# A hybrid decoder step: projected tiles turned to rows in 32x32 blocks by VectorE and moved to their lanes by GpSimd, the convolution's first product on ScalarE

## The reference

```python
n = rmsnorm(h, g);  u = n @ w_in            # columns: z | xBC | dt | q | k | v
xbc_ext  = concatenate([conv_prev, xbc], axis=1)
new_conv = xbc_ext[:, -3:]                  # an output
xbc_act  = silu(b + sum(xbc_ext[:, j:j + L] * w[j] for j in range(4)))
y = ssd_chunked(x * dt, dt, A, B, C, state) + d_skip * x     # x | B | C = xbc_act
y = rmsnorm_by_group(y * silu(z)) * ssd_norm
o = rmsnorm(dilated_attention(q, k, v))     # k and v of the new tokens are outputs
h = h + concatenate([y, o]) @ w_out
h = h + moe(rmsnorm(h))                     # top 4 of 32 experts, clamped SwiGLU
return rmsnorm(h)
```

## Time and profile before

| | us |
|---|---|
| median of 3 runs | 1232.03 (1231.84 to 1236.32) |
| the profiled execution, first to last instruction | 1232.7 |
| TensorE busy (PE) | 1160.5 (94%) |
| VectorE busy (DVE) | 365.5 (30%) |
| ScalarE busy (ACT) | 250.0 (20%) |
| GpSimd busy (POOL) | 55.2 (4%) |
| chain that ended last | PE 57%, DMA 38%, DVE 2% |
| DMA | 463.58 MB, mean 376 GB/s |

### The profile page before, as it was taken

One profiled execution on the slowest core, in us unless ns is written; L12 is line 12 of the kernel. 1 busy time (PEld: TensorE's weight loads), 2 busy tenths in 40 slices (PEclk: granted clock), 3 DMA queues, 4 the chain that ended last, 5 costly groups with the idle time before them and its releaser, 6 DMA issues.

```text
span 1232.7 us, 14855 instructions
## 1 busy us (share of the span) xinstructions
PE 1160.5 (94%) x5867; PEld 506.8 (41%) x5882; DVE 365.5 (30%) x752; ACT 250.0 (20%) x496; POOL 55.2 (4%) x49
## 2 busy tenths in 40 slices
PE   9999999899999999999989898989898989898997
PEld 6777656534433434333333333333232323232332
DVE  2457335765512132221203030303122121212122
ACT  2014443627320211112011111111111111020113
POOL 0000032621000000000000000000000000000000
PEclk9999999999999999999999999999999999999999
DMA  9677557379799999999999999999999999999995
GB/s 293 207 250 256 205 183 280 135 254 417 326 426 430 426 427 430 427 430 428 427 430 428 426 431 428 427 430 429 429 429 427 429 428 427 430 427 428 429 427 247
DMA packets 64368, 463.58 MB, mean 376 GB/s; under 512 B 7704, under 2 KB 25268, under 8 KB 38380
## 3 DMA queue, kind: packets, MB, share of 16 engines
q1 hardware_dynamic: 62206, 459.02, 90.5%
q10 hardware_dynamic: 1582, 2.22, 0.5%
q0 software_dynamic: 544, 1.84, 0.4%
HBM read 455.82 MB, written 7.24 MB: 376 GB/s over the span
## 4 chain that ended last, share of the span: by engine, by line
PE 57%; DMA 38%; DVE 2%; issue 1%; ACT 1%; SPq 0%; DVEq 0%; ACTq 0%
DMA ring<-in_w 34%; PE ps L2436 21%; PE ps L1909 10%; PE ps L2460 5%; DMA own<-in_w 3%; PE ps L2354 2%; PE ps L2362 2%; PE ps L2323 2%; PE ps L2356 1%; PE ps L2194 1%; PE ps L1951 1%; PE ps L2372 1%; PE ps L2422 1%; PE ps L1985 1%; PE ps L1928 1%
## 5 line engine op out<-in xcount | busy, mean ns | idle before, releaser
L2436 PE MATMUL ps<-ring,own 128*64 128x512 f32 x1456 | 326.5, 595 | 31.4 <-DMA ring<-in_w 31.4
L2436 PEld LDWEIGHTS ps<-ring,own 128*64 128x64 f32 x1456 | 104.1, 137 | 236.0 <-issue 178.3
L1763 DVE TENSOR_SCALAR own<-ps 128x512 f32<-128x512 f32 x32 | 22.1, 692 | 556.8 <-PE ps L2436 556.8
L2436 PE MATMUL ps<-own 128*64 128x512 f32 x592 | 134.1, 594 | 11.8 <-DMA own<-in_w 11.8
L2460 PE MATMUL ps<-ring,own 128*64 128x512 f32 x592 | 133.5, 595 | 5.4 <-issue 5.2
L1909 PE MATMUL ps<-own,ring 128*128 128x288 f32 x512 | 131.4, 412 | 0.0
L1909 PEld LDWEIGHTS ps<-own,ring 128*128 128x128 f32 x512 | 96.1, 192 | 29.2 <-issue 4.5
L2460 PE MATMUL ps<-own 128*64 128x512 f32 x432 | 98.4, 595 | 3.9 <-issue 2.6
L2436 PEld LDWEIGHTS ps<-own 128*64 128x64 f32 x592 | 43.2, 137 | 95.1 <-issue 84.5
L2460 PEld LDWEIGHTS ps<-ring,own 128*64 128x64 f32 x592 | 44.0, 137 | 82.9 <-issue 72.5
L1151 ACT ACTIVATE own<-ps 64x512 f32<-64x512 f32 x60 | 35.5, 592 | 205.6 <-PE ps L2460 204.8
(11 more groups left out here) (384 smaller groups left out, 1003.1 us busy)
## 6 DMA issues: line engine op xcount, KB each, us to landing
ring<-in_w SPq DMA_DIRECT2D x128, 2048.0 KB, 38.6
own<-in_w SPq DMA_DIRECT2D x63, 2048.0 KB, 37.4
ring<-in_w_in SPq DMA_DIRECT2D x16, 1024.0 KB, 7.7
ring<-in_cache_win_k SPq DMA_DIRECT2D x8, 1024.0 KB, 5.8
ring<-in_cache_win_v SPq DMA_DIRECT2D x8, 1024.0 KB, 4.9
ring<-in_w_out SPq DMA_DIRECT2D x6, 1024.0 KB, 10.9
ring<-in_state_ssm SPq DMA_DIRECT2D x8, 512.0 KB, 7.3
out_ssm_sample<-ring SPq DMA_DIRECT2D x8, 512.0 KB, 8.6
```

Source lines behind the costliest of these rows:

```text
L1763: nc.vector.tensor_scalar(xg_o, hid[:, 0], LIMIT, None, ALU.min).then_inc(sem("glu_ready"), 1)
L2436: last = nc.tensor.matmul(ps[C * half:C * half + C, 1 + m, :], xT[:, k, C * u:C * u + C], rows[:, D * half + 512 * m:D * half + 512 * m + ...
```

## The change

- The `nat` and `conv_out` steps go: 26 times three transposes and three times four on TensorE, with their copies out of bank 2, and the waits for this bank.
- A `turn` step, or for v and z the copy out of the projection itself, is one VectorE transpose in 32x32 blocks of a 128x288 tile, into `turned_tiles` (room for two pairs of tiles). k is turned from `kT`, x and B from `xbcT` after SiLU, v and z straight from PSUM.
- After a block transpose each 32x32 block is right in itself but stands on the lanes of its columns. `blocks_to_rows` on GpSimd takes a pair of tiles and copies the blocks to the lanes of their tokens: for each of 4 groups of lanes 4 copies of 128 elements per lane and one of 64. There are 13 pairs. It signals `natural`, and VectorE waits for it before it fills the room of the pair two before.
- The convolution tails are one VectorE transpose (`tails`, 128x768) and eight GpSimd copies of 384 elements per lane.
- All x, B and C projections are copied out by ScalarE, all v and z by VectorE.
- The convolution's first product is an activation on ScalarE (scale and bias by lane), ahead of VectorE's three additions.

```diff
+TURNED = [n for n, (kind, i, _) in enumerate(TILES) if n % 2 == 0 and (kind in "kvz" or (kind == "x" and i < 10))]
+OUT_ON_DVE = [n for n, (kind, i, _) in enumerate(TILES) if kind in "vz" or (kind in "qk" and n % 2)]
+OUT_ON_ACT = [n for n in range(NT) if n not in OUT_ON_DVE]
@@ mixer_steps
         proj(9 + 2 * b)
-        back(7 + 2 * b if b < 3 else 2 * b + 5)
         steps.extend(("silu", i) for i in convs)
+        steps.extend(("turn", 12 + i) for i in convs)
@@ GpSimd
+            def blocks_to_rows(n):
+                what, j, _ = TILES[n]
+                rows, j = {"k": (k_nat, j), "v": (v, j), "z": (z, j), "x": (xs, j)}[what]
+                if what == "x" and j >= 8:
+                    rows, j = Bn, j - 8
+                pair = 2 * (TURNED.index(n) % 2)
+                if what in "vz":
+                    wait_proj_out(pool, n + 1)
+                else:
+                    pool.wait_ge(sem("blocks_ready"), sum(1 for m in TURNED if m <= n and TILES[m][0] in "kx"))
+                for i in range(4):
+                    lanes = slice(32 * i, 32 * i + 32)
+                    for q in range(4):
+                        to = rows[32 * q:32 * q + 32, 0:2, j * P:(j + 2) * P].rearrange("p c (t r) -> p c t r", t=2)[:, :, :, lanes]
+                        nc.gpsimd.tensor_copy(to, turned_tiles[lanes, pair:pair + 2, 0:SEQ].rearrange("p t (c q r) -> p q c t r", c=2, q=4)[:, q])
+                    last = nc.gpsimd.tensor_copy(rows[0:NS, 2, j * P:(j + 2) * P].rearrange("p (t r) -> p t r", t=2)[:, :, lanes], turned_tiles[lanes, pair:pair + 2, SEQ:TOK])
+                last.then_inc(sem("natural"), 1)
+                pool.wait_ge(sem("natural"), TURNED.index(n) + 1)
+            for name, src, ns in (("k", k_nat, (4, 6)), ("v", v, (8, 10))):
+                for n in ns:
+                    blocks_to_rows(n)
...
+            for n in range(12, 22, 2):
+                blocks_to_rows(n)
+            pool.wait_ge(sem("kv_out"), 64)
+            pool.wait_ge(sem("tails_ready"), 1)
...
+            pool.wait_ge(sem("score_ps"), DB)
+            blocks_to_rows(24)
+            blocks_to_rows(26)
             pool.wait_ge(sem("dt_ready"), 1)
...
+            blocks_to_rows(28)
...
             pool.wait_ge(sem("w_used"), NT // 2)
             decays_in(0)
...
+            blocks_to_rows(30)
             pool.wait_ge(sem("silu_ready"), CT)
@@ ScalarE
+                elif kind == "conv":
+                    wait_proj_out(act, 12 + i)
...
+                    nc.scalar.activation(conv_t[:, i % 2, :], xbcP[:, i, 0:XC], ACT.Identity, scale=cw[:, i, 24:25], bias=cw[:, i, 28:29]).then_inc(sem("conv_begun"), 1)
@@ VectorE
+                        moved = TURNED.index(i - i % 2) - 1
+                        if i % 2 == 0:
+                            dve.wait_ge(sem("natural"), moved)
+                        nc.vector.transpose(d3(turned_tile(i), 32), d3(src, 32)).then_inc(sem("proj_out_dve"), 1)
+                elif kind == "turn":
+                    what, j, _ = TILES[i]
+                    if i % 2 == 0 and TURNED.index(i) > 1:
+                        dve.wait_ge(sem("natural"), TURNED.index(i) - 1)
+                    if what == "x":
+                        dve.wait_ge(sem("silu_ready"), j + 1)
+                        src = xbcT[:, j, :]
...
+                    ins = nc.vector.transpose(d3(turned_tile(i), 32), d3(src, 32))
@@ VectorE, conv
-                    link(nc.vector.tensor_scalar(t, xbcP[:, i, 0:XC], cw[:, i, 24:25], cw[:, i, 28:29], ALU.mult, ALU.add))
@@ TensorE, nat
-                    turn_waits()
-                    turn[:] = [kind, i]
-                    for c in range(3):
-                        last = nc.tensor.transpose(ps[0:ROWS[c], 2, c * P:(c + 1) * P], src[:, cols(c)], ident)
-                    last.then_inc(sem("nat_ps"), 1)
```

More of the change, by code:

```diff
@@ L157, in mixer_steps @@
 def mixer_steps():
-    steps, nat = [], 0
+    steps = []
     def proj(n):
         steps.append(("proj", n))
-    def back(last, most=1):
-        nonlocal nat
-        for _ in range(most):
-            if nat < len(NAT) and NAT[nat] <= last:
-                steps.append(("nat", nat))
-                nat += 1
     for n in range(8):
         proj(n)
-        back(n - 2)
         if n == 4:
             steps.append(("qrep", 0))
+        if n == 6:
+            steps.extend([("turn", 4), ("turn", 5)])
     for b in range(DB):
@@ L181, in mixer_steps @@
         if b == 0:
-            steps.append(("krep", 0))
-        back(6 + 2 * b if b < 3 else 2 * b + 5)
+            steps.extend([("krep", 0), ("turn", 6), ("turn", 7)])
         steps.extend(("conv", i) for i in convs)
@@ L207, in mixer_steps @@
     steps.extend(("exp", i) for i in range(4, 8))
-    steps.extend([("silu", 10), ("silu", 11), ("conv_out", 0)])
+    steps.extend([("silu", 10), ("silu", 11), ("tails", 0)])
     steps.extend(("pv", t) for t in range(3))
     proj(26)
-    steps.extend([("conv_out", 1), ("ptrans", 4), ("ptrans", 5), ("conv_out", 2)])
-    back(24)
+    steps.extend([("ptrans", 4), ("ptrans", 5)])
     proj(27)
@@ L246 @@
 STEPS = mixer_steps()
-NAT_ON_DVE = [i for i in range(len(NAT)) if i < 8 and i % 2 == 0]
-NAT_ON_ACT = [i for i in range(len(NAT)) if i not in NAT_ON_DVE]
 def ring_items():
@@ L733, in _ @@
+            pool.wait_ge(sem("tails_ready"), 1)
+            for i in range(4):
+                for q in range(2):
+                    last = nc.gpsimd.tensor_copy(conv_o[32 * q:32 * q + 32].rearrange("p (m r) -> p m r", m=CT)[:, :, 32 * i:32 * i + 32], tails[32 * i:32 * i + 32, :, q, :])
+            last.then_inc(sem("conv_o"), 1)
+            pool.wait_ge(sem("conv_o"), 1)
+            pool.wait_ge(sem("score_ps"), DB)
+            blocks_to_rows(24)
+            blocks_to_rows(26)
             dA = dts[:, 48:96]
@@ L735, in _ @@
             pool.wait_ge(sem("dt_ready"), 1)
-            pool.wait_ge(sem("conv_out_ps"), 3)
-            for i in range(8, 18):
-                wait_nat_out(pool, i)
             for c in range(3):
@@ L1865, in old_round @@
                 if r == 0:
-                    for n in range(len(NAT)):
-                        wait_nat_out(pe, n)
                     pe.wait_ge(sem("Qz_ready"), 3)
@@ L1988, in _ @@
                     if i == 0:
-                        for n in range(4, 8):
-                            wait_nat_out(pe, n)
+                        wait_natural(pe, "v")
                     for b in range(4):
@@ L2011, in _ @@
                     last.then_inc(sem("dt_ps"), 1)
-                elif kind == "conv_out":
-                    wait_proj_out(pe, 14 + 4 * i)
-                    wait_proj_out(pe, 15 + 4 * i)
-                    turn_waits()
-                    turn[:] = [kind, i]
-                    for m in range(4):
-                        last = nc.tensor.transpose(ps[0:59, 2, m * P:(m + 1) * P], xbcP[:, 4 * i + m, XS0 - 3:XP], ident)
-                    last.then_inc(sem("conv_out_ps"), 1)
                 elif kind == "p_score":
```

130 lines of the change are left out of this document (36 added, 94 removed).

## The result

The changed kernel takes 1226.21 us (median of 4 runs, 1223.19 to 1227.56), the kernel before beside it 1232.9 us (4 runs, 1231.84 to 1236.32): a ratio of 0.9934 with a 95% interval of [0.9917, 0.9951]. By the ratio that is 8.1 us faster (6.0 to 10.2 by the interval); the two medians differ by 6.7 us, the spans of the two profiled executions by 7.0. The forecast was 1220.5 us, 11.6 us faster, with 1218 to 1223.5 as its own band and a range of 1215 to 1230. The measured median lies in the wide range and not in the band.

What follows compares the result with a forecast made beforehand. The expert-weight stream sets the end and starts when the mixer, bound by TensorE's order to 200 us, frees buffers. Savings 5.4 + 4.4 + 0.6 + 1.7 = 12.1, less 0.5 for GpSimd, give 1220.5 us, range 1215 to 1230.

Steps and rivals of the forecast that it cites:

- Sixteen turns at 0.335 us: TensorE before 129 us: 16 of the 26 turns, three transposes each, go and save 5.4 us.
- The waits for the shared bank: TensorE behind 129 us: waits for ScalarE over the single bank of all turns go, together 4.4 us.
- The turn beside the softmax: One later TensorE turn costs 1.35 us with its wait; 0.6 counted, since the softmax transposes need ScalarE too.
- Five turns of 0.335: Five of TensorE's last seven turns cost 0.335 us each, 1.7 us saved.
- the wait is hidden: Sample loop: VectorE's block transposes wait for ScalarE's SiLU, but TensorE wants the next keys only 9.85 us later.
- the second block transpose end 2.6 us after the odd projection: Sample loop: a copy and two SiLUs on ScalarE, then VectorE's transpose, end 2.6 us after the odd projection.
- the zeroed tile: GpSimd's memset ends at 190.3 us, VectorE's copy into its tile is due at 189.8; 0.5 us charged.
- Charging nothing: VectorE and GpSimd contending for SBUF: copies lie mostly under one-input key transposes, so no time is charged.
- A: Rival: GpSimd's queue gives part of the gain back, memset late by 2.9 to 10 us; 1226 us, chance 0.18.
- B: Rival: GpSimd becomes the bound, gain gone at 10.7 us a pair; 1245 us at 0.60 us a copy, chance 0.09.
- C: Rival: the saving isn't passed on, as something unmoved releases the first expert weights; 1232 us, chance 0.06.
- D: Rival: more is saved, the last turn, the whole 1.35 us and shorter shared-bank waits; 16 us, 1216, chance 0.05.

Runs made afterwards that it cites:

- e5: The kernel before with only the convolution's first product moved to ScalarE, turns left on TensorE: 1235.12 us against 1233.98, ratio 1.0015.
- e1: The changed kernel with VectorE taking the prompt's maxima ahead of the six convolution additions at sample 4: 1222.85 us, ratio 0.9894 to the kernel before.
- e9: The changed kernel with VectorE's block transposes moved behind the next sample's key transposes: 1225.71 us, ratio 0.9935 to the kernel before.
- e6: The changed kernel with the convolution's first product back on VectorE: 1228.16 us, ratio 0.9955 to the kernel before.
- e11: The changed kernel with 8 GpSimd copies instead of 20 for each x pair, giving other numbers there: 1225.93 us, ratio 0.9931 to the kernel before.
- e4: The changed kernel with maxima ahead of the additions, GpSimd's last z pair later, three unused TensorE products: 1223.21 us, ratio 0.9899 to the kernel before.
- e8: The changed kernel with maxima ahead of sample 4's additions and three unused TensorE products ahead of its wait: 1222.8 us, ratio 0.9917.

## Why the prediction was right, and where its sizes were off

**The size.** The direction, the mechanism and the wide range came true; the size did not. Of 11.6 us some 7 to 8 arrived, and 1226.21 us lies even above 1225.9, below which the forecast laid 0.77 of its chances. That the wide range held it is in part luck: what was lost by the wait and the low clock below stood in no term of the sum. Another part of the distance to 1220.5 us is the base: it was the median of three runs, 1232.03 us, and 37 later runs of that kernel have a median of 1234.09.

**The direction and the mechanism.** Time left TensorE's chain with the turns, and reached the end: at the second old round the changed kernel's profile is 6.9 us earlier (214.27 against 221.13), at its end 7.0. From that round to the end it is 1011.6 us before and 1011.4 after. Step by step, up to the last pattern product of the prompt (199.18 before, 189.60 after, 9.6 us earlier where 12.1 was forecast):

- Sixteen turns at 0.335 us, 5.4 us forecast. The score products are 9.39 to 9.40 us apart, as forecast, and the twelve turns between the first and the eighth are worth 3.9 us. The four ahead of them gave only 0.89 us in this pair of profiles. The start differs more than that between executions, though, and it goes with the granted clock of the stretch 10 to 20 us: with the turns moved the first score product stands at 54.2 to 54.6 us where that clock is 1.00, at 55.6 to 56.3 where it is 0.83, at 57.2 and 57.6 where it is 0.66. With the turns on TensorE it stands at 56.18 at a clock of 1.00 (e5) and at 57.14 at 0.83, so 0.9 to 2.0 us later than its likes. The shortfall of 0.45 us can't be told from that.
- The waits for the shared bank, 4.4 us forecast: from 129.27 to 150.97 are 21.70 us before, from 125.70 to 143.10 are 17.40 after, 4.3 us.
- The turn beside the softmax, 0.6 us forecast: from 161.98 to 169.34 before and 153.72 to 160.99 after only 0.09 us went. The transposes next to it need ScalarE as well: the second waits 0.97 us, and the first, which did not wait before, now waits 0.62. The doubt was right, the half kept was too much.
- Five turns of 0.335, 1.7 us forecast, 1.6 measured.
- Not forecast: the wait of 1.20 us at the prompt's maxima. This is the step that failed. It read "the wait is hidden because TensorE wants the next keys only 9.85 us later". That is true of the keys. In sample 4 VectorE's queue also holds the maxima behind the additions, and TensorE wants those at the end of the odd projection, at 94.02 us, 8.1 us after the score product's end (85.95). VectorE's queue starts 1.0 us behind that end, at the SiLU, and takes 8.2 us, to 95.16. With the maxima in front (e1) 1.5 us come back. The queue's late start has a cause that the forecast left out too: it had the second block transpose end 2.6 us after the odd projection, and in sample 3 it ends 3.3 us after (84.51 to 87.81), with ScalarE loading a table for 1.28 us ahead of the SiLU. VectorE waits 1.96 and 3.01 us at the SiLUs with such a load ahead, and 0.49 us at most at those without. It is not the whole cause: with VectorE taken off this wait (e9) TensorE's is still 0.98 us.
- Behind the last pattern product of the prompt: TensorE's wait ahead of the pattern product costs 0.2 us more than before, and the stretch with the low clock, 22.66 us against 20.13, gives back 2.5. This is the largest term that the forecast did not have.

**VectorE and ScalarE.** The block transpose has a median of 0.448 us, and 0.45 was the estimate. ScalarE stayed far from its limit. That the first product helps VectorE is shown by e6; that it brings nothing alone, by e5.

**GpSimd.** A pair at 6.2 us was forecast, 6.3 measured; 0.287 and 0.226 us a copy with 0.04 between. It was late for the zeroed tile by 0.33 us (VectorE's wait there), with 0.5 forecast (0.4 by the forecast's own sum, which took off 12.2 us there where it had 12.1). The memset itself came at 191.13 and not at 188.5, because the decay that it follows came with a later last projection.

**Contention.** Charging nothing was right for the time (without most of the copies, in e11, the distance to the last projection is 0.15 us shorter). The row shows who pays: VectorE's additions keep 0.55 us each, GpSimd's copies rise from 0.32 to about 0.52; beside the key transposes they keep 0.32. SBUF — State Buffer in the Trainium skill, section Who interferes with whom, calls the ports that the two engines share an exclusive lock, and has a VectorE instruction with two SBUF inputs contend with a GpSimd instruction that reads SBUF. The trace agrees on GpSimd's side (2.08 us against 1.27 for four copies); a hold-up of VectorE by the copies is not seen (3.30 us against 3.27). It is seen elsewhere: in the kernel before L1473 takes 1.52 us at 224.16, beside a tensor_tensor of GpSimd (223.11 to 225.13), and 0.68 at best. So which engine pays is not settled by these runs for other pairs of instructions.

**The clock.** At full clock the change brings 1229.8 - 1220.3 = 9.5 us (± 0.3) against 11.6 forecast, and e1 11.3 us (from the heights before rounding). Between the measured spans it is less, since the mean clock is lower: (0.9972 - 0.9953) x 1000 x 0.94 = 1.8 us, which leaves 7.7. In the profiles the stretch from the pattern product to the second old round shows it: 18.93 and 19.12 us in e1 and e6, where the clock held, 20.13 before with its short drop, 22.66 in the changed kernel, twice. The forecast took the stretch behind 200 us as only moved. The mean clock of a run also has the low stretch at 10 to 20 us in it, so it is not a measure of this place alone: e1's profiled execution has 0.996 and lost nearly all of that at the start. Why the low clock comes in one execution and not in another stays open: the same wait of 0.96 us stands ahead of it in e1 and e6, which kept the clock.

**The rivals.** A named the time best (1226), but for another reason, so by luck: it had GpSimd give back 2.9 to 10 us, and VectorE's wait for GpSimd was a third of a microsecond. B's condition, 10.7 us a pair, was not reached even with twice the copies (8.7). C is refuted, the gain at the second old round arrived at the end. D's larger saving was not there: the turn beside the softmax gave 0.09 us of its 1.35, the shared bank 4.3, and the last turn nothing.

**The best version.** e1 is one line's move and at full clock 1.8 us (± 0.5) faster than the change; e4 and e8 are not told apart from it.

## What to carry to other kernels

Work that is taken off the critical engine pulls its next demands forward, so look at each thing that this engine asks of the others at its new time, the rare ones (here a reduction in one sample of eight) first of all, and order each helper's queue by these demands. A helper with 3 us to spare per period can take many small copies. Where a program's runs differ by 4 us at one place, put span against granted clock before reading a 2 us effect from a median.

## What the hardware showed that was not expected

- Copies of 64 elements on 32 lanes start 0.22 us apart on GpSimd, closer than their listed 0.229 us; of 128 elements 0.33 us apart at 0.287. Halving a copy raised a pair by 2.4 us, or 0.12 us for each copy added.
- Beside VectorE's two-input additions a GpSimd copy of 128 elements takes about 0.2 us longer, and VectorE's additions hardly any (3.30 to 3.37 us for six against 3.27 to 3.32).
- A granted clock of 0.50 for 10 us in the middle of a busy stretch, in two executions of the same kernel at the same place, and absent in two kernels (e1, e6) that have the same wait ahead of it.
